# Seven RMS norms on one NeuronCore: the last square summed on its own, one root for four PSUM banks, weight parts moved, and most unread products of TensorE left out

## The chip, the cores and the metric

One Trainium2 chip, one of its NeuronCores. The metric is the device time of one launch in microseconds; lower is better. TensorE multiplies, VectorE and ScalarE do the elementwise work, SyncE issues the loads.

## The reference, cut to what matters

Two networks of two layers each follow one another on 512 rows of 1024 features (a context of 256 rows runs beside the first one). All is float32. The norms that this case is about are these:

```python
# first block, per layer l (modulate = RMS norm over the 1024 features, gain, scale and shift)
x = x + gt1 * merge_branches(...)                                  # w_o
x = x + gt2 * sq_relu_mlp(modulate(x, g_norm2[l], sh2, sc2), w_ff1[l], w_ff2[l])
...                                                                # the same for ctx_s in layer 0
# second block, per layer
h = _rmsnorm(x, pre_mix_g[layer]);  h = mixer(h)
x = x + _rmsnorm(h, post_mix_g[layer])
h = _swiglu(_rmsnorm(x, pre_ffn_g[layer]), w_gate, w_up, w_down)
x = x + _rmsnorm(h, post_ffn_g[layer])

def _rmsnorm(x, g):
    y = x * lax.rsqrt(jnp.mean(x * x, axis=-1, keepdims=True) + EPS)
    return y * g
```

A norm needs every feature of a row before it gives its first value, so each of them stands between two stretches of products.

## The kernel before, in words

Activations lie with their features on the 128 partitions: `x` is eight blocks (`KB` = 8) of 128 features by 512 rows, `xc` the same with 256 rows. A float32 product is made of three: each operand is split into a rounded upper part and a lower part, and `three` multiplies upper by upper, upper by lower and lower by upper. Weights come as tiles of 128x1024, in the order in which they are used. Four buffers hold them (`R` = 4): SyncE loads `raw`; ScalarE writes `w_hi` (`split(c)` does it for tile c + 3); VectorE writes `w_lo` (`lower_w(c)`, also for tile c + 3), which frees `raw` for the next load; TensorE then multiplies the tile into one of the four PSUM banks of `ring` (`product`, L1681 to L1683). Each engine runs its own instruction list in order and waits on semaphores; `plan()` fixes the order of the steps.

A norm after a stretch of products goes like this. The last tile of the stretch is added to `x` by VectorE (`residual`, L3006, or L3382 in the second block's feed-forward part). VectorE squares the block (L2655), adds the square to the running sum in `scr` block 2 (L2656) and tells TensorE (`squares_done`, L2659). TensorE sums over the partitions by one-column products: for each of four slices of 128 rows the slice of `scr` is the stationary operand and a column of ones the moving one (`column_sums`, L1752; in `last_norm` L2266 and in `mixed_norm` L2283 the sum and the last square are summed by products of their own, two groups of four). The profile counts each float32 product of this kind as two. ScalarE takes four roots, one for each slice's bank (`column_roots`, L932). VectorE takes the reciprocal (L2609). TensorE spreads it over the partitions by four products with the identity (`spread_rstd`, L1759). VectorE scales the first block (L2637, L3318 or L3100), ScalarE writes its upper part, VectorE its lower part (L2645, L3322), and the first product of the next stretch follows; the other blocks follow in the same pipeline.

While the chain of small steps runs, TensorE is given products that nobody reads (`keep_warm`, L1724, 128x512 each). `WARM`, `WARM_MIXED` and `WARM_POST` say how many stand before the sums, after them, and after the spread.

The places, in order of time (us of the profiled execution, end of the last product before the norm):

- 293: `norm2` of the context, layer 0 (`column_norm`, 256 rows). TensorE also has to sum and spread what `x`'s first norm needs here (L1802, L1740).
- 892 and 1683: `norm2` of the main rows, layers 0 and 1 (`column_norm`).
- 2040: `pre_mix` of layer 0 (`column_norm`).
- 2239 and 2868: `post_mix` (`mixed_norm`). Here ScalarE squares the tiles itself (L1091) and copies them (L1092), then splits the next weight tile (L894), loads the table of the root (`root_table`, L936) and takes the roots.
- 2610: `post_ffn` of layer 0 (`last_norm`), and 3238: `post_ffn` of layer 1, with which the kernel ends.

Two more sums stand between products: in `kv_norm1` (1272) and before the main rows' first norm ("roots", 485).

The loops of `w_o` and of `ff` on VectorE are hardware loops (`grouped`), with addresses worked out in registers in `w_o`.

```python
for kind, layer, stream, first in steps: ...
    elif kind == "post_ffn":           last_norm(first, ring[:, 0, :] if layer else bank[0])
    elif kind in ("norm2", "pre_mix"): column_norm(first, length(stream), summed(kind, layer, stream), bank[0], stream == "ctx")
    elif kind == "post_mix":           mixed_norm(layer, first)
```

Of the kernel before, what the change touches and what calls it, by code (L numbers as in the profile page):

```python
# [6 lines left out]
F32 = mybir.dt.float32  # L7
# [57 lines left out]
WARM, WARM_MIXED, WARM_POST = (11, 4, 8), (0, 9, 11), (2, 9, 11)  # L65
# [3 lines left out]
PAD = 16  # L69

# [308 lines left out]
def build(nc, ws, vecs, mats, ropes, x_in, ctx_in, bv_in, out, upto=None):  # L379
# [5 lines left out]
    with ExitStack() as stack:  # L385
# [42 lines left out]
        bank = [stack.enter_context(nc.psum_tensor(f"bank{i}", [P, SEQ], F32)) for i in range(4, 8)]  # L428
# [454 lines left out]
        def _(act):  # L883
# [750 lines left out]
            for n, (kind, layer, stream, first) in enumerate(steps):  # L1634
# [20 lines left out]
                elif kind == "norm2":  # L1655
                    norm(layer, stream, first, 3)
                elif kind == "pre_mix":
                    gain_norm(first, layer == 0)
                elif kind in ("post_mix", "post_ffn"):
                    post_norm(first)  # L1660
# [15 lines left out]
        def _(pe):  # L1676
# [49 lines left out]
            def column_norm(first, T, is_summed, spread, with_x):  # L1726

                keep_warm(first, WARM[0])
                column_sums(T, is_summed, 2)
                keep_warm(first, WARM[1])  # L1730
                C.next(root_ready, T // P)
# [12 lines left out]
            def column_sums(T, is_summed, at_block, done=ss_ready):  # L1744
                for k in range(1 if is_summed else KB):
                    if is_summed:
                        pe.wait_ge(s_acc, C.next(s_acc))
                    else:
                        pe.wait_ge(sq_ready, C.next(sq_ready))
                    src = scr[:, at_block if is_summed else k % 2, :]  # L1750
                    for tt in range(T // P):
                        m = nc.tensor.matmul(bank[tt][:, 0:1], src[:, tt * P:(tt + 1) * P], ones[:, 0:1],  # L1752
                                             start=k == 0, stop=is_summed or k == KB - 1)
                    m.then_inc(done, 1)
# [12 lines left out]
            def first_mod():  # L1767
# [9 lines left out]
                for t in range(FIRST):  # L1777
# [11 lines left out]
                    if t == KB + 3:  # L1789
                        pe.wait_ge(s_bv, 16)  # L1790
                        column_sums(CTX, True, 0)
                        C.next(root_ready, CTX // P)
# [43 lines left out]
            def kv_norm1(first):  # L1836
# [5 lines left out]
                column_sums(SEQ, True, 2)  # L1842
                C.next(root_ready, SEQ // P)
# [416 lines left out]
            def last_norm(first, spread):  # L2260

                keep_warm(first, WARM_POST[0])
                for part in range(2):
                    pe.wait_ge(s_acc, C.next(s_acc))
                    for tt in range(4):
                        m = nc.tensor.matmul(bank[tt][:, 0:1], scr[:, 2 + part, tt * P:(tt + 1) * P], ones[:, 0:1],  # L2266
                                             start=not part, stop=bool(part))
                m.then_inc(ss_ready, 1)
                keep_warm(first, WARM_POST[1] if first < n_tiles else 3)
                C.next(root_ready, 4)  # L2270
# [4 lines left out]
            def mixed_norm(layer, first):  # L2275
# [11 lines left out]
                C.next(root_ready, 4)  # L2287
# [31 lines left out]
            def ml_in(first):  # L2319
                four_abreast(first)  # L2320
                column_sums(SEQ, True, 2)
                C.next(root_ready, 4)
# [12 lines left out]
            def ffn(layer, first):  # L2335
                four_abreast(first)
                for u in range(4, FFN_TILES):
# [3 lines left out]
                    if pos < 2 * n:  # L2341
                        product(c, SEQ, h_hi, h_lo)
                        if u == 4:
                            column_sums(SEQ, True, 2)
                            C.next(root_ready, 4)
# [155 lines left out]
            for kind, layer, stream, first in steps:  # L2501
# [4 lines left out]
                elif kind == "roots":  # L2506

                    pe.wait_ge(root_ready, C.now(root_ready))
                    column_sums(length(stream), True, summed_at(kind, layer, stream), s_ctx_sum)
                    C.next(root_ready, length(stream) // P)  # L2510
                elif kind == "post_ffn":
                    last_norm(first, ring[:, 0, :] if layer else bank[0])
                elif kind in ("norm2", "pre_mix"):

                    column_norm(first, length(stream), summed(kind, layer, stream), bank[0], stream == "ctx")
# [29 lines left out]
        def _(dve):  # L2545
# [54 lines left out]
            def column_rstd(T, kept=None):  # L2600
                if kept is None:
                    dve.wait_ge(root_ready, C.next(root_ready, T // P))
# [7 lines left out]
                C.next(s_rstd)  # L2610
                dve.wait_ge(s_rspread, C.next(s_rspread))
# [37 lines left out]
            def add_squares(src, T, start=False, at_block=2):  # L2649
# [6 lines left out]
                step(nc.vector.tensor_tensor(total, total, scr[:, 3, :T], ALU.add))  # L2656

# [351 lines left out]
            def w_o(layer, stream, first):  # L3009
                T = length(stream)  # L3010
                step(nc.vector.memset(scr[:, 2, :T], 0.0))

                def body(c, u, off):
                    lower_w(c, off)
                    add_squares(residual(c, u, off, off, layer, stream, 2), T)
                grouped(dve, KB, first, body, C, {post: R, dve_own: 2 * R})
                squares_done()

            def ff(layer, stream, first):
# [54 lines left out]
                def body(c, u, off, between=None):  # L3074
# [17 lines left out]
                else:  # L3092
                    grouped(dve, 64, first, body, C, {evac: KB, dve_own: 4 * KB - 1, post: 2 * KB}, size=16)
                squares_done()
# [16 lines left out]
            def mix_out(layer, first):  # L3111
# [10 lines left out]
                lower_w(first + KB)  # L3122
# [190 lines left out]
            def residual_parts(i, first, mixed, gain):  # L3313

                column_rstd(SEQ)
# [23 lines left out]
            def ffn(layer, first):  # L3339
# [4 lines left out]
                dve.wait_ge(root_ready, C.next(root_ready, 4))  # L3344
# [20 lines left out]
                for u in range(4, FFN_TILES):  # L3365
                    c = first + u
                    pos, n = (u % 24, 8) if u < 48 else (u - 48, 6)
                    if u > 6:
                        lower_w(c)
                    done(c)  # L3370
# [10 lines left out]
                    else:  # L3381
# [3 lines left out]
                        elif u >= 48:  # L3385
                            squares_done()
                            step(nc.vector.tensor_tensor(scr[:, 3, :], z[:, m, :], z[:, m, :], ALU.mult))
                squares_done()
# [19 lines left out]
            def ml_in(first):  # L3408
                i = deferred("ml_in", 1)
                lower_w(first)  # L3410
# [3 lines left out]
                dve.wait_ge(root_ready, C.next(root_ready, 4))  # L3414
# [217 lines left out]
            for kind, layer, stream, first in steps:  # L3632
# [5 lines left out]
                elif kind == "norm1" and (layer, stream) == (0, "ctx"):  # L3638
                    dve.wait_ge(root_ready, C.next(root_ready, CTX // P))
                    norm(0, "ctx", 0)  # L3640
                    step(nc.vector.tensor_copy(v_bias[:, :], bias_columns))
                elif kind == "roots":
                    C.next(root_ready, length(stream) // P)
# [57 lines left out]
```

## Time and profile before

| | |
|---|---|
| median of 3 runs | 3254.96 us (3254.74 to 3256.89) |
| time of the profiled execution | 3257.88 us |
| its span | 3256.1 us |
| TensorE products | 3191.3 us busy, 98% of the span, 16081 instructions |
| TensorE weight loads | 2682.4 us, 82% |
| VectorE | 2096.6 us, 64% |
| ScalarE | 1236.7 us, 38% |
| mean granted clock of TensorE | 0.991 of full speed |

The span is what the profiler saw from the first instruction to the last; 1.8 us of the launch lie outside it. "Busy" of TensorE counts the unread products and the weight loads that its products wait for, so 98% is not work that the reference asks for.

### The profile page before, as it was taken

How to read it: one execution, taken by the hardware profiler on the slowest of the kernel's cores; microseconds unless marked ns; L12 is line 12 of the kernel's file. 1: busy time of each engine (PE TensorE's matmuls, PEld its weight loads, DVE VectorE, ACT ScalarE, POOL GpSimd, SP SyncE). 2: the span in 40 equal slices, each digit the busy share in tenths (PEclk: the TensorE clock that was granted, in tenths of full speed). 3: DMA queues.
4: the chain of work that ended last, by engine and by line, in shares of the span. 5: the costliest groups of instructions: out<-in, count | busy, mean ns of one | idle time of the engine just before them, and what ended most of it. 6: DMA issues, size and time to landing. Idle time of an engine off the chain costs nothing.

```text
span 3256.1 us, 42822 instructions
## 1 busy us (share of the span) xinstructions
PE 3191.3 (98%) x16081; PEld 2682.4 (82%) x16081; DVE 2096.6 (64%) x2925; ACT 1236.7 (38%) x1828; POOL 0.2 (0%) x4
## 2 busy tenths in 40 slices
PE   8899999999999999999999999999999999999998
PEld 6889998887888888888788888888888878888886
DVE  6777886655687778656475655875544676664446
ACT  4654435454232223555332222535222266542221
POOL 0000000000000000000000000000000000000000
PEclk9999999999999999999999999999999999999999
DMA  7654552211334553211222222222222336223222
GB/s 270 198 188 155 179 189 89 68 56 65 116 130 136 173 185 114 100 56 52 78 84 97 101 98 95 80 97 78 97 93 98 107 71 88 69 77 105 97 97 72
DMA packets 100716, 358.18 MB, mean 110 GB/s; under 512 B 11208, under 2 KB 12368, under 8 KB 100560
## 3 DMA queue, kind: packets, MB, share of 16 engines
q1 hardware_dynamic: 98864, 352.85, 31.7%
q10 hardware_dynamic: 1696, 3.16, 2.0%
q8 instruction: 108, 1.77, 0.2%
q14 instruction: 48, 0.39, 0.0%
HBM read 351.76 MB, written 2.10 MB: 109 GB/s over the span
## 4 chain that ended last, share of the span: by engine, by line
PE 90%; DVE 5%; ACT 2%; issue 1%; DMA 0%; DVEq 0%; ACTq 0%; SPq 0%
PE ring L1681 26%; PE ring L1683 25%; PE ring L1682 25%; PE bank L1681 2%; PE bank L1683 2%; PE bank L1682 2%; DVE w_lo L2576 1%; ACT w_hi L894 1%; PE ring L2009 1%; PE ring L2010 1%; PE bank L2034 1%; PE bank L2035 1%; PE ring L1980 1%; DVE x L3327 0%; PE bank L2165 0%
## 5 line engine op out<-in xcount | busy, mean ns | idle before, releaser
L1681 PE MATMUL ring<-h_hi,w_hi 128*128 128x512 f32 (+1 forms) x2776 | 1028.7, 371 | 16.3 <-DVE h_lo L2645 8.5
L1683 PE MATMUL ring<-h_hi,w_lo 128*128 128x512 f32 (+1 forms) x2776 | 1020.3, 368 | 0.0
L1682 PE MATMUL ring<-h_lo,w_hi 128*128 128x512 f32 (+1 forms) x2776 | 1020.3, 368 | 0.0
L2576 DVE TENSOR_TENSOR w_lo<-raw,w_hi 128x1024 fp32r<-128x1024 f32 x598 | 730.8, 1224 | 319.2 <-ACT w_hi L894 301.8
L894 ACT ACTIVATE w_hi<-raw 128x1024 fp32r<-128x1024 f32 x598 | 630.4, 1056 | 707.9 <-PE ring L1683 667.5
L1681 PEld LDWEIGHTS ring<-h_hi,w_hi 128*128 128x128 f32 x2776 | 529.5, 191 | 109.8 <-issue 14.4
L1683 PEld LDWEIGHTS ring<-h_hi,w_lo 128*128 128x128 f32 x2776 | 528.6, 190 | 86.0
L1682 PEld LDWEIGHTS ring<-h_lo,w_hi 128*128 128x128 f32 x2776 | 529.6, 191 | 82.8
L1681 PE MATMUL ring<-y_hi,w_hi 128*128 128x512 f32 (+1 forms) x1456 | 540.0, 371 | 11.7 <-DVE z L2860 7.7
L1683 PE MATMUL ring<-y_hi,w_lo 128*128 128x512 f32 (+1 forms) x1456 | 536.3, 368 | 0.0
L1682 PE MATMUL ring<-y_lo,w_hi 128*128 128x512 f32 (+1 forms) x1456 | 536.0, 368 | 0.0
L1681 PEld LDWEIGHTS ring<-y_hi,w_hi 128*128 128x128 f32 x1456 | 275.8, 189 | 60.9 <-DVE z L2860 10.2
L1683 PEld LDWEIGHTS ring<-y_hi,w_lo 128*128 128x128 f32 x1456 | 275.9, 189 | 45.6
L1682 PEld LDWEIGHTS ring<-y_lo,w_hi 128*128 128x128 f32 x1456 | 276.0, 190 | 44.1 <-issue 0.5
L1596 ACT ACTIVATE scr<-ring 128x512 f32<-128x512 f32 (+1 forms) x96 | 50.5, 526 | 302.7 <-PE ring L1683 300.1
L3081 DVE TENSOR_TENSOR z<-scr 128x512 f32<-128x512 f32 (+1 forms) x96 | 57.4, 598 | 125.4 <-ACT scr L1596 125.1
L3006 DVE SCALAR_TENSOR_TENSOR x<-ring,mod,x 128x512 f32<-128x512 f32 (+1 forms) x80 | 60.0, 751 | 118.4 <-PE ring L1683 118.4
L2882 DVE TENSOR_REDUCE mx<-ring 128x1 fp32r<-128x768 f32 (+1 forms) x80 | 67.9, 849 | 61.9 <-PE ring L2010 61.4
L2892 DVE TENSOR_TENSOR y_lo<-z,y_hi 128x512 fp32r<-128x512 f32 (+1 forms) x112 | 72.2, 646 | 48.9 <-ACT y_hi L1507 47.8
L1133 ACT ACTIVATE scr<-scr 128x512 f32<-128x512 f32 x40 | 25.3, 632 | 196.6 <-DVE scr L3374 196.6
L1507 ACT ACTIVATE y_hi<-bank 128x512 fp32r<-128x512 f32 (+1 forms) x112 | 63.4, 566 | 75.0 <-PE bank L1683 74.0
L1500 ACT ACTIVATE z<-bank 128x512 f32<-128x512 f32 (+1 forms) x112 | 63.6, 568 | 54.8 <-PE bank L2035 52.5
(382 smaller groups left out, 3104.0 us busy)
## 6 DMA issues: line engine op xcount, KB each, us to landing
raw<-ws SPq DMA_DIRECT2D x606, 512.0 KB, 3.3
z<-ws SPq DMA_DIRECT2D x52, 512.0 KB, 4.4
x<-ws SPq DMA_DIRECT2D x4, 512.0 KB, 9.7
x<-x_t SPq DMA_DIRECT2D x1, 2048.0 KB, 11.3
out_t<-x SPq DMA_DIRECT2D x8, 256.0 KB, 2.0
z<-xc ACTq DMA_DIRECT2D x6, 256.0 KB, 11.3
xc<-ctx_t SPq DMA_DIRECT2D x1, 1024.0 KB, 12.7
z<-ropes ACTq DMA_DIRECT2D x2, 512.0 KB, 4.3
```

Of the source, the lines that this page charges most:

```text
L894: nc.scalar.activation(w_hi[:, t % R, :], raw[:, t % R, :], ACT.Copy).then_inc(w_hi_ready, 1)
L1500: nc.scalar.activation(z[:, 13 + k % 2, :T], bank[k % 2][:, :T], ACT.Exp, scale=HEAD ** -0.5)\
L1507: nc.scalar.activation(y_hi[:, 4 + k % 2, :T], bank[k % 2][:, :T], ACT.Exp, scale=HEAD ** -0.5)\
L1596: nc.scalar.activation(scr[:, u % 2, :T], ring[:, c % R, :T], ACT.Relu).then_inc(evac, 1)
L1681: nc.tensor.matmul(o, a_hi, b_hi, start=start, stop=False)
L1682: nc.tensor.matmul(o, a_hi, b_lo, start=False, stop=False)
L1683: return nc.tensor.matmul(o, a_lo, b_hi, start=False, stop=stop)
L2576: nc.vector.tensor_tensor(w_lo[:, u, :], raw[:, u, :], f(w_hi[:, u, :]), ALU.subtract).then_inc(w_ready, 1)
L2882: nc.vector.reduce_max(mx[:, h % 2, qt:qt + 1], view[:, 0:n_kt * P], AX_X).then_inc(s_max, 1)
L2892: nc.vector.tensor_tensor(y_lo[:, b, :T], src, f(y_hi[:, b, :T]), ALU.subtract).then_inc(s_p, 1)
L3006: step(nc.vector.scalar_tensor_tensor(o, ring[:, c % R, :T], g, o, ALU.mult, ALU.add), post)
L3081: step(nc.vector.tensor_tensor(z[:, m % 2, :T], scr[:, m % 2, :T], scr[:, m % 2, :T], ALU.mult))
```

## The change: what it does, and the diff

1. **Last square.** In `w_o`, in `ff` and in the feed-forward part `ffn`, the last block's square is no longer added to the sum. `last_squares` writes it to `scr` block 3 and signals; `squares_done` is moved ahead of the last residual. TensorE sums block 2 and block 3 by products of their own (`part_sums`, twice), the first group before the last square is there.
2. **One root.** The four banks become one PSUM tensor, and `column_roots` is one instruction over a column of each bank, with one increment of `root_ready`.
3. **Weight parts.** In `post_mix`, `root_table` moves ahead of the wait for the last tile, and `split(first)` moves behind the root. In `residual_parts`, `lower_w(first)` stands between the reciprocal and the wait for the spread.
4. **Unread products.** `WARM` goes from (11, 4, 8) to (0, 0, 4), `WARM_MIXED` from (0, 9, 11) to (0, 0, 5), `WARM_POST` from (2, 9, 11) to (0, 0, 5), and the three after the last sums of the kernel become one: 155 products before, 30 after.
5. **`w_o`** is written out instead of looped, and its sum starts with the first square instead of a memset.

```diff
-WARM, WARM_MIXED, WARM_POST = (11, 4, 8), (0, 9, 11), (2, 9, 11)
+WARM, WARM_MIXED, WARM_POST = (0, 0, 4), (0, 0, 5), (0, 0, 5)
+FF_SQUARES = 7
...
-        bank = [stack.enter_context(nc.psum_tensor(f"bank{i}", [P, SEQ], F32)) for i in range(4, 8)]
+        banks = stack.enter_context(nc.psum_tensor("bank4", [P, 4, SEQ], F32))
+        bank = [banks[:, i, :] for i in range(4)]
...
             def column_roots(T, cols=root_cols):
-                for tt in range(T // P):
-                    nc.scalar.activation(cols[:, tt:tt + 1], bank[tt][:, 0:1], ACT.Sqrt, bias=eps[:, 0:1],
-                                         scale=1.0 / D).then_inc(root_ready, 1)
+                n = T // P
+                nc.scalar.activation(cols[:, 0:n].rearrange("p (a b) -> p a b", b=1), banks[:, 0:n, 0:1], ACT.Sqrt,
+                                     bias=eps[:, 0:1], scale=1.0 / D).then_inc(root_ready, 1)
...
-            def post_norm(first):
-                root_table()
+            def post_norm(first, mixed):
+                if not mixed:
+                    root_table()
                 act.wait_ge(ss_ready, C.next(ss_ready))
                 column_roots(SEQ)
+                if mixed:
+                    split(first)
...
                     if layer or u:
                         split(c)
+                    if u == KB - 1:
+                        root_table()
                     done(c)
...
-                split(first + KB)
...
-            def column_norm(first, T, is_summed, spread, with_x):
+            def column_norm(first, T, squares_before, spread, with_x):
+                part_sums(T, 2, squares_before, True, False)
                 keep_warm(first, WARM[0])
-                column_sums(T, is_summed, 2)
+                part_sums(T, 3, 1, False, True).then_inc(ss_ready, 1)
                 keep_warm(first, WARM[1])
...
+            def part_sums(T, at_block, after, start, stop):
+                pe.wait_ge(s_acc, C.next(s_acc, after))
+                for tt in range(T // P):
+                    m = nc.tensor.matmul(bank[tt][:, 0:1], scr[:, at_block, tt * P:(tt + 1) * P], ones[:, 0:1],
+                                         start=start, stop=stop)
+                return m
...
# kv_norm1, and the same for "roots"
                 product(first, CTX, h_hi, h_lo, before=blocks_ready(k0))
-                column_sums(SEQ, True, 2)
+                part_sums(SEQ, 2, FF_SQUARES, True, False)
+                part_sums(SEQ, 3, 1, False, True).then_inc(ss_ready, 1)
...
             def last_norm(first, spread):
+                part_sums(SEQ, 2, 1, True, False)
                 keep_warm(first, WARM_POST[0])
-                for part in range(2): ...
+                m = part_sums(SEQ, 3, 1, False, True)
                 m.then_inc(ss_ready, 1)
-                keep_warm(first, WARM_POST[1] if first < n_tiles else 3)
+                keep_warm(first, WARM_POST[1] if first < n_tiles else 1)
...
-            def column_rstd(T, kept=None):
+            def column_rstd(T, kept=None, between=None):
...
                 nc.vector.reciprocal(rstd_cols[:, :T // P], roots[:, :T // P]).then_inc(s_rstd, 1)
                 C.next(s_rstd)
+                if between:
+                    between()
                 dve.wait_ge(s_rspread, C.next(s_rspread))
...
+            def last_squares(src, T):
+                nc.vector.tensor_tensor(scr[:, 3, :T], src, src, ALU.mult).then_inc(s_acc, 1)
...
             def w_o(layer, stream, first):
                 T = length(stream)
-                step(nc.vector.memset(scr[:, 2, :T], 0.0))
-                def body(c, u, off):
-                    lower_w(c, off)
-                    add_squares(residual(c, u, off, off, layer, stream, 2), T)
-                grouped(dve, KB, first, body, C, {post: R, dve_own: 2 * R})
-                squares_done()
+                for u in range(KB):
+                    lower_w(first + u)
+                    if u < KB - 1:
+                        add_squares(residual(first + u, u, 0, 0, layer, stream, 2), T, start=u == 0)
+                    else:
+                        squares_done()
+                        last_squares(residual(first + u, u, 0, 0, layer, stream, 2), T)
...
# ff, tile 15 of each group of 16; ffn, its last tile, likewise
+                        if m == 2 * KB - 1:
+                            squares_done()
                         o = residual(c, m - KB, off, 0, layer, stream, 5)
-                        add_squares(o, T, start=m == KB)
+                        if m == 2 * KB - 1:
+                            last_squares(o, T)
+                        else:
+                            add_squares(o, T, start=m == KB)
...
# residual_parts (VectorE); mix_out and ml_in lose their own lower_w
-                column_rstd(SEQ)
+                column_rstd(SEQ, between=lambda: lower_w(first))
```

## Rows read from the trace of the kernel before

**Rows 1.** The page's head: span and instructions.

```profile
span 3256.1 us, 42822 instructions
```

**Rows 2.** Groups by line: busy us, mean ns of one, idle before it and releaser.

```profile
L932 ACT ACTIVATE small<-bank,eps 128x1 f32<-128x1 f32 x50 | 9.1, 264 | 62.2 <-PE bank L1752 41.4 <-PE bank L2266 20.8
...
L2655 DVE TENSOR_TENSOR scr<-x 128x512 f32<-128x512 f32 (+1 forms) x72 | 49.8, 692 | 2.5
```

**Rows 3.** The chain, norm2 of layer 0: start us, us, what.

```profile
892.62 0.25 PE ring L1683
...
893.12 0.76 DVE x L3006
...
895.60 1.05 PE bank L1752 x8
...
897.73 1.17 PE bank L1759 x8
...
898.92 0.76 DVE scr L2637
```

**Rows 4.** The chain, pre_mix of layer 0.

```profile
2040.07 2.56 PE ring L1724 x11
...
2045.91 0.76 DVE scr L2637
```

**Rows 5.** The chain, post_mix of layer 0.

```profile
2240.27 0.59 ACT z L1092
2240.86 0.94 ACT w_hi L894
...
2241.82 1.28 ACT L936
...
2245.39 0.76 DVE z L3318
```

**Rows 6.** The chain, post_mix of layer 1.

```profile
2868.49 1.74 PE bank L2283 x16
...
2873.36 0.76 DVE z L3318
```

**Rows 7.** The chain, post_ffn of layer 0.

```profile
2610.10 0.25 PE ring L1683
...
2614.85 1.23 DVE w_lo L2576
...
2617.42 0.76 DVE z L3318
```

**Rows 8.** The chain, post_ffn of layer 1, the kernel's end.

```profile
3238.11 0.25 PE ring L1683
...
3243.41 0.75 DVE z L3100
```

**Rows 9.** The chain, norm2 of the context.

```profile
294.26 2.68 PE ring L1724 x11
...
298.75 0.89 PE bank L1740 x8
```

**Rows 10.** The chain, the last add before "roots" and the sums in kv_norm1.

```profile
486.38 0.44 DVE scr L2656
...
1272.59 0.79 PE bank L1752 x8
```

**Rows 11.** Stretches: busy us by engine (instructions), then TensorE's granted clock, DMA share, GB/s.

```profile
2195.10:2198.50 3.40, 3.40 (x32) 3.40 (x32) 0.00 (x0) 0.37 (x1) 0.00 (x0) 1.00 0.00 0
2199.00:2202.40 3.40, 3.40 (x10) 2.62 (x9) 0.18 (x1) 1.55 (x3) 0.00 (x0) 0.50 0.00 0
...
2610.30:2620.60 10.30, 8.38 (x47) 6.36 (x45) 5.64 (x9) 2.91 (x7) 0.00 (x0) 1.00 0.31 103
...
1277.40:1280.80 3.40, 1.08 (x5) 0.93 (x6) 3.27 (x5) 1.92 (x3) 0.00 (x0) 1.00 0.05 20
1280.80:1284.20 3.40, 3.40 (x10) 2.63 (x9) 3.40 (x7) 1.63 (x3) 0.00 (x0) 0.50 0.02 5
```

More of the change, by code:

```diff
@@ L1659, in _ @@
                 elif kind in ("post_mix", "post_ffn"):
-                    post_norm(first)
+                    post_norm(first, kind == "post_mix")
                 elif kind == "ab":
@@ L1742, in x_spread @@
                 m.then_inc(s_x_spread, 1)
[L1744 to L1754, printed above, removed]
+            def part_sums(T, at_block, after, start, stop):
[4 more added lines that the diff above has]
+                return m
             def spread_rstd(T, spread):
@@ L1790, in first_mod @@
                         pe.wait_ge(s_bv, 16)
[L1791 to L1792 removed]
+                        part_sums(CTX, 0, 1, True, True).then_inc(ss_ready, 1)
+                        C.next(root_ready)
                         nc.tensor.matmul(bias_columns, bias_rows, ident[0:8, 0:8], start=True, stop=True)
@@ L2260, in last_norm @@
             def last_norm(first, spread):
+                part_sums(SEQ, 2, 1, True, False)
                 keep_warm(first, WARM_POST[0])
[L2263 to L2267, printed above, removed]
+                m = part_sums(SEQ, 3, 1, False, True)
                 m.then_inc(ss_ready, 1)
-                keep_warm(first, WARM_POST[1] if first < n_tiles else 3)
-                C.next(root_ready, 4)
+                keep_warm(first, WARM_POST[1] if first < n_tiles else 1)
+                C.next(root_ready)
                 spread_rstd(SEQ, spread)
@@ L2286, in mixed_norm @@
                 keep_warm(first, WARM_MIXED[1])
-                C.next(root_ready, 4)
+                C.next(root_ready)
                 spread_rstd(SEQ, bank[0])
@@ L2320, in ml_in @@
                 four_abreast(first)
-                column_sums(SEQ, True, 2)
-                C.next(root_ready, 4)
+                part_sums(SEQ, 2, 1, True, True).then_inc(ss_ready, 1)
+                C.next(root_ready)
                 for u in range(4, 10):
@@ L2343, in ffn @@
                         if u == 4:
-                            column_sums(SEQ, True, 2)
-                            C.next(root_ready, 4)
+                            part_sums(SEQ, 2, 1, True, True).then_inc(ss_ready, 1)
+                            C.next(root_ready)
                         if u == 5:
@@ L2508, in _ @@
                     pe.wait_ge(root_ready, C.now(root_ready))
-                    column_sums(length(stream), True, summed_at(kind, layer, stream), s_ctx_sum)
-                    C.next(root_ready, length(stream) // P)
+                    part_sums(length(stream), 2, FF_SQUARES, True, False)
+                    part_sums(length(stream), 3, 1, False, True).then_inc(s_ctx_sum, 1)
+                    C.next(root_ready)
                 elif kind == "post_ffn":
@@ L2513, in _ @@
                 elif kind in ("norm2", "pre_mix"):
-                    column_norm(first, length(stream), summed(kind, layer, stream), bank[0], stream == "ctx")
+                    column_norm(first, length(stream), 1 if kind == "norm2" else FF_SQUARES, bank[0], stream == "ctx")
                 elif kind == "post_mix":
@@ L3092, in ff @@
                 else:
-                    grouped(dve, 64, first, body, C, {evac: KB, dve_own: 4 * KB - 1, post: 2 * KB}, size=16)
-                squares_done()
+                    grouped(dve, 64, first, body, C, {evac: KB, dve_own: 4 * KB - 3, post: 2 * KB}, size=16)
             def post_norm(gain_of):
@@ L3343, in ffn @@
                     lower_w(first + u)
-                dve.wait_ge(root_ready, C.next(root_ready, 4))
+                dve.wait_ge(root_ready, C.next(root_ready))
                 nc.vector.reciprocal(rstd_cols[:, :], root_cols[:, :]).then_inc(s_rstd, 1)
@@ L3413, in ml_in @@
                     lower_w(first + u)
-                dve.wait_ge(root_ready, C.next(root_ready, 4))
+                dve.wait_ge(root_ready, C.next(root_ready))
                 nc.vector.reciprocal(rstd_cols[:, :], root_cols[:, :]).then_inc(s_rstd, 1)
@@ L3638, in _ @@
                 elif kind == "norm1" and (layer, stream) == (0, "ctx"):
-                    dve.wait_ge(root_ready, C.next(root_ready, CTX // P))
+                    dve.wait_ge(root_ready, C.next(root_ready))
                     norm(0, "ctx", 0)
@@ L3642, in _ @@
                 elif kind == "roots":
-                    C.next(root_ready, length(stream) // P)
+                    C.next(root_ready)
                 elif kind == "norm1":
```

14 lines of the change are left out of this document (6 added, 8 removed).

## The prediction, made before the changed kernel had run

> **What bounds the kernel now.** I read the page's head first, for the span [rows 1]; then the groups by line, for what a root and a square cost [rows 2]; then the chain of waits around each norm, because a mean over the kernel says nothing of places that take 8 us each. The reader is to see one pattern there: the last product ends, a chain of small steps crosses VectorE, TensorE, ScalarE, VectorE, TensorE, VectorE, and only then the next product can start. Outside the norms TensorE multiplies without a gap, so a microsecond taken out of such a chain is a microsecond of the kernel, and a microsecond anywhere else is nothing. Last I read the stretches in which TensorE's granted clock was low [rows 11].
>
> Where the chain shows L1724, TensorE ran unread products while it had nothing else. A step that follows such a piece by 0.04 us was in general released by another engine, not by TensorE. Norm2 of the context is different: eleven unread products fill 294.26 to 296.94, and its sums stand behind them in TensorE's list [rows 9].
>
> **The change part by part.** Durations are those of one execution, of 3257.88 us, whose span is 3256.1 [rows 1]; the median of the runs is 3254.96, 2.9 us under it. The sum is a difference, made against the profiled execution and then taken off the median.
>
> The new chain, from the end of the last product to VectorE's first scaling, for 512 rows: 0.04 for the wait, residual 0.76 [rows 3], wait 0.02, square 0.70 [rows 2], 0.06 to TensorE, four slices summed 1.05 [rows 3], 0.08 to ScalarE, one root 0.26 [rows 2], 0.03, reciprocal 0.19, 0.04, spread 1.17 [rows 3], 0.02. That is 4.42 us. One root over four banks isn't in the trace: at least the 0.26 of one bank, at most the 0.7 of four in a row; I take 0.26, because it still writes so few columns.
>
> - Norm2 of both layers: in layer 0 the last product ends at 892.87 and the scaling starts at 898.92, 6.05 us [rows 3]. Gone are the add with its wait, the loop's end and its address registers (together 1.2) and three roots (0.45). Gain 1.6, and the same in layer 1: **3.2**.
> - Pre_mix: 2040.07 to 2045.91, 5.84 us [rows 4]; `ff` had no address registers on this way. **1.4**.
> - Post_mix of layer 0: the square and the copy (0.59) of the last tile lead to 2240.86; then ScalarE splits a weight tile (0.94) and loads the root's table (1.28) before it takes the roots, and VectorE scales at 2245.39 [rows 5]. The last product ended about 0.5 us before the copy began at 2240.27, at 2239.75, so this is 5.64. In the new order the table load lies under the products of the last tile, since ScalarE has nothing to do there; without that cover it costs its 1.28 again. ScalarE squares (0.6), TensorE sums (to 1.7), the root is there at 2.0. Now something else is late: ScalarE splits until 3.1, and VectorE, which has taken `lower_w(first)` in ahead of its wait for the spread, works on it until 4.33 (1.23 for such a piece [rows 7]). The spread is ready at 3.5 and waits. 4.35, gain **1.3**. Queued behind the piece on VectorE are the scalings, so the whole next stretch waits for it.
> - Post_mix of layer 1: the table was loaded already, and the way was 2868.49 to 2873.36, 4.87 us [rows 6]. The new one is the same 4.35: **0.5**.
> - Post_ffn of layer 0: from 2610.35 to 2617.42, 7.07 us [rows 7]. `lower_w` stood ahead of the reciprocal here, which had to wait for 2616. Sixteen records of sums become eight behind the last square. New: root at 2.8, split until 3.9, VectorE's piece until 5.13, scaling at 5.15. **1.9**.
> - Post_ffn of layer 1: 3238.36 to 3243.41, 5.05 us [rows 8]; new 4.33. **0.7**.
> - Norm2 of the context: from the end of L1802 at 294.26 to the end of the spread at 298.75, 4.5 us [rows 9]. With 256 rows each step is about half: two groups of sums 1.0, root and reciprocal 0.6, spread 0.55. Gain **2.3**, most of it the unread products that stood in the way.
> - "Roots": the add of 0.44 [rows 10] with its wait and the loop's end go from VectorE's way to the first norm of the main rows. **0.7**.
> - Kv_norm1: here the sums stand between two tiles of products and the squares were long there. A second group of eight records costs TensorE its 0.8 [rows 10] to 0.9. **Minus 0.9**.
>
> The deferred norms of `ffn` and `ml_in` get one root for four, with TensorE at products meanwhile: nothing. The writing-out of `w_o` but for its last tile, and the adds that `ff` saves in its first three groups, lie under products of 5.5 us a tile: nothing. The next load of a weight tile waits for `lower_w`; its transfer is needed many products later and is hidden before and after.
>
> Sum: 3.2 + 1.4 + 1.3 + 0.5 + 1.9 + 0.7 + 2.3 + 0.7 − 0.9 = 11.1 us.
>
> **What the missing unread products cost.** The granted clock never fell in one of the changed places: across the longest of them, post_ffn of layer 0, TensorE was busy for 8.38 of 10.30 us, and the clock stayed at full [rows 11]. It fell elsewhere: after 3.4 us in which TensorE ran only one-column sums (32 records) the next 3.4 us were at half, 1.2 instead of 2.4 GHz; and after 3.4 us with 1.08 us of work (a spread's end and five records in all) it fell as well [rows 11]. In a slow stretch TensorE made ten products, at 0.43 us each; at full clock they are 0.23, so a slow stretch that lies wholly on products costs about 1.7 us (fifteen would have fitted).
>
> After the change, the way from the last product to the spread holds nothing but one-column sums for 3.2 us (norm2, pre_mix, post_ffn), 2.3 us (post_mix) and about 2.4 us (context). Then come the spread and its four or five unread products, some 2 us at work. Behind them the first product still waits for VectorE and ScalarE's first block: 1.7 us at norm2 and pre_mix, 3.2 at post_mix and post_ffn. So each of seven places has one or two stretches like those [rows 11]. The lower bound is nothing: the clock holds. The upper is two slow stretches each, 3.3 us. At norm2 and pre_mix a fall would mostly lie on the spread and on waiting, with 0.5 to 1 us to pay; behind post_mix and post_ffn it would lie on products. I take 0.9 us a place: about four full slow stretches in all, 4 × 1.65 = 6.6, less what is hidden. **Minus 6.3.** The rows nearest to it (3.4 us of sums, and 2.3 us of idling in 3.4, both followed by a fall) are a little longer than most of the new gaps, hence not seven.
>
> The clock fell behind both such stretches [rows 11]. By the Trainium skill ("TensorE: Matmul & The Clock Gate", Part 1: The HAM clock gate) the throttled state is the default and only activity releases it. Taken alone, that rule speaks against this change: it would have all seven places fall once, 7 × 1.65 = 11.6 instead of 6.3, and the sum would be 0.5 us slower.
>
> Net: 11.1 − 6.3 = 4.8 us faster. Against the profiled 3257.9 that is 3253.1; against the median, 3254.96 − 4.8 = **3250.2 us**.
>
> **The rivals.**
> 1. The clock holds in most places (none to two falls). For it: the products just before and after each place are dense, and a place that was idle for 2 us of 10 kept its clock. Against it: the falls, both in the same rows [rows 11]. Then 8 to 11 us are gained: **3245**.
> 2. The clock falls everywhere, in some places for two stretches. Mechanism: the gap slows the spread to half, TensorE finds too little to do in the slow stretch itself and stays slow into the next products. It decides from 11.1 / 7 = 1.6 us a place: below that the change gains, above it loses. With two stretches at half of the places, 11 × 1.65 = 18: 7 us slower, **3262**. With one each: 3255.5, no change. For it, the fall after 1.08 us of work in 3.4 [rows 11]; against it, that the spread and its four or five unread products stand in the middle of each gap.
> 3. The chain gets shorter on paper only: ScalarE's one root over four banks costs as much as four (7 × 0.45 = 3.2), and the piece of `lower_w` comes later than I put it. Then the gain is about 8 gross, less the clock's 6.3: **3253**.
>
> **How the numbers follow.** The forecast (three to five falls, 3 to 7 us gained) 0.52; rival 1 0.25; rival 2 0.13, of which 0.05 at the slow end; rival 3 0.10. 0.2% is 6.5 us, about what a measurement of this kernel can tell from no change. Faster than 3248.4: rival 1 and the forecast's best tenth, 0.33. Slower than 3261.5: rival 2's end and a little for what I don't see, 0.06. The rest, 0.61, lies within. The range of 8 in 10 goes from rival 1 (3244.5) to the one-fall-each case with its spread (3257).
>
> **What would show it.** In the changed kernel's chain: sums starting 1.6 us after the last product of norm2 (2.7 before); one L932-like root of 0.26 per norm; scaling 4.4 us after the last product at norm2 and pre_mix, 4.35 at both post_mix, 5.15 at post_ffn of layer 0; at post_mix and post_ffn VectorE's w_lo piece as the last link ahead of the scaling; 16 records of sums in kv_norm1. In the granted clock: about four low stretches more than now, with products of 0.43 us behind post_mix and post_ffn. I am wrong if the new places show no low stretch (then it is rival 1), if slow products follow all of them (rival 2), or if a scaling starts later than said although the clock held (rival 3).

## The result and the profile after

The changed kernel took 3260.81 us in the median of 22 runs (3248.45 to 3267.41), the kernel before 3254.91 (3253.07 to 3258.85, 22 runs). The ratio is 1.0014, with a 95% interval of 1.0007 to 1.0020: slower by 0.14%. Measured once more with the experiments it took 3255.19 us (12 runs, 3248.68 to 3262.59) beside 3255.07, ratio 1.0003 (0.9993 to 1.0013). Both lie under the 0.2% that the prediction called the limit of what can be told from no change; faster it is not, and 4.8 us faster was forecast. One run of kernel 2 below (8154.78 us) and one of the kernel before (8256.51 us) stand far outside all others and count in no ratio or mean.

The runs of the changed kernel spread over 19 us (14 in the second set), those of before over 6 (7 to 12 beside the later experiments). Each run lists its span and the mean granted clock of TensorE, from which its time at the low clock follows: (1 − clock) × 2 × span. In the runs of the kernel before that were made beside the experiments it is 52 to 65 us nearly always, with a mean of 57; in those of the changed kernel 78 to 131 us, mean 111 (mean 99 in the second set). Over 21 of the 22 runs (one lists a clock that no time fits) a straight line, 3223.7 us + 0.32 × the time at the low clock, follows the run's time with a correlation of 0.97. Both kept profiles of the changed kernel are of quick runs: 3253.18 us with 98 us at the low clock, and 3248.68 with 78 in the second set. No run with the 117 us of the median was profiled. What follows is the first of the two. The page's head, its line of products and its line of roots:

```profile
span 3251.4 us, 42456 instructions
...
PE 3177.9 (98%) x15996; PEld 2676.0 (82%) x15996; DVE 2084.6 (64%) x2904; ACT 1231.8 (38%) x1792; POOL 0.2 (0%) x4
```

```profile
L936 ACT ACTIVATE small<-bank,eps 128x4 f32<-128x4 f32 (+1 forms) x14 | 3.7, 263 | 58.4 <-PE bank L1757 57.1 <-PE bank L2286 1.3
```

One root over four banks takes 263 ns, as one over a single bank did [rows 2]. The chain of waits at norm2 of layer 0, which answers to [rows 3] (start us, us, what):

```profile
887.70 0.24 PE ring L1691
887.94 0.02 issue
887.97 0.76 DVE x L3016
...
888.75 0.70 DVE scr L2666
889.45 0.14 issue
889.59 1.34 PE bank L1757 x8
...
891.50 0.14 issue
891.63 2.06 PE bank L1764 x8
...
893.72 0.76 DVE scr L2643
...
896.15 0.76 PE ring L1689
...
900.33 0.32 PE ring L1689
```

The sums begin 1.65 us after the last product, as the prediction had it. But the spread takes 2.06 us instead of 1.17, the sums 1.34 instead of 1.05, and the scaling starts 5.78 us after the last product: 4.42 were forecast, 6.05 it was. The granted clock tells why. Stretches of the changed kernel (columns as in [rows 11]):

```profile
886.80:890.10 3.30, 2.42 (x18) 2.17 (x17) 1.44 (x2) 0.00 (x0) 0.00 (x0) 1.00 0.50 159
890.30:893.50 3.20, 2.48 (x12) 2.42 (x13) 0.18 (x1) 0.26 (x1) 0.00 (x0) 0.50 0.00 0
893.70:896.90 3.20, 2.43 (x6) 1.45 (x6) 3.05 (x5) 1.58 (x3) 0.00 (x0) 0.50 0.00 0
897.10:900.30 3.20, 3.20 (x9) 2.48 (x8) 3.20 (x6) 1.76 (x3) 0.00 (x0) 0.50 0.02 5
```

The clock fell to 1.2 GHz while the one-column sums ran, stayed there through the spread and the gap behind it, and only rose when products had run for over 4 us, from 896.15 to 900.3, at 0.43 us each. That is one slow stretch of 10.2 us at one norm.

Where the clock held, or fell too late to matter, the chain is nearly what was forecast. Pre_mix, against [rows 4]:

```profile
2037.15 1.04 PE bank L1757 x8
...
2038.27 0.27 ACT small L936
...
2038.89 1.14 PE bank L1764 x8
2040.03 0.03 issue
2040.06 0.76 DVE scr L2643
```

From the last product at 2035.50 that is 4.56 us (before 5.84; forecast 4.42). TensorE, idle now, starts 0.14 us after its release, where 0.06 and 0.04 were forecast. Post_mix of layer 0, against [rows 5], 4.25 us from the last product at 2232.29, with VectorE's weight piece as the last link:

```profile
2232.29 1.75 PE bank L2286 x16
...
2234.23 1.05 ACT w_hi L898
...
2235.31 1.23 DVE w_lo L2580
2236.54 0.70 DVE z L3331
```

Post_mix of layer 1 took 4.26 us (against [rows 6]). The clock did fall at both, at 2235.0 and 2866.4 and for 3.4 us each, but behind the sums, and VectorE's weight piece ends after the slowed spread. In layer 0 the clock was back at 2238.4 and the first product started at 2239.71: that fall cost nothing. Post_ffn of layer 0 and the kernel's end, against [rows 7, 8]:

```profile
2601.47 0.70 DVE z L3397
...
2604.96 2.06 PE bank L1764 x8
2607.01 0.02 issue
2607.04 0.76 DVE z L3331
```

```profile
3234.64 1.40 PE bank L1757 x8
3236.04 0.64 PE ring L1732
3236.67 2.02 PE ring L1764 x8
3238.69 0.02 issue
3238.72 1.41 DVE z L3114 x2
```

At post_ffn of layer 0 the spread at the low clock ends at 2607.01 and has become the last link, in place of the weight piece; the scaling comes 5.6 us after the last product (forecast 5.15). At the end the scaling comes 5.67 us after the last product, later than the 5.05 of before, because sums and spread ran at the low clock. The one unread product runs there at about twice its time, but the reciprocal ends only at 3236.55 and the spread starts at once behind it (3236.60): the product isn't what holds the chain up. Kv_norm1 shows the second group of sums on TensorE (before 0.79, [rows 10]):

```profile
1267.75 1.68 PE bank L1757 x16
```

All stretches below 1 make 100 us in this profile, 62 in the one before.

### The profile page after: what moved, and what is told of

Its sections match the earlier page's. It is cut to its first block, busy times and chain, and to the rows that moved or that the text cites. A ratio compares the mean times of both kernels' runs of the same rounds, so it can differ in the third digit from the quotient of the medians.

```text
span 3251.4 us, 42456 instructions
## 1 busy us (share of the span) xinstructions
PE 3177.9 (98%) x15996; PEld 2676.0 (82%) x15996; DVE 2084.6 (64%) x2904; ACT 1231.8 (38%) x1792; POOL 0.2 (0%) x4
## 4 chain that ended last, share of the span: by engine, by line
PE 90%; DVE 5%; ACT 2%; issue 1%; DMA 0%; DVEq 0%; ACTq 0%; SPq 0%
PE ring L1689 26%; PE ring L1690 26%; PE ring L1691 26%; PE bank L1689 2%; PE bank L1691 2%; PE bank L1690 2%; DVE w_lo L2580 1%; ACT w_hi L898 1%; PE ring L2015 1%; PE ring L2016 1%; PE bank L2040 1%; PE bank L2041 1%; PE ring L1986 1%; PE bank L2171 0%; DVE z L2983 0%
## 5 line engine op out<-in xcount | busy, mean ns | idle before, releaser
L3016 DVE SCALAR_TENSOR_TENSOR x<-ring,mod,x 128x512 f32<-128x512 f32 x80 | 60.1, 751 | 121.0 <-PE ring L1691 121.0
```

The source lines that it names most:

```text
L3016: step(nc.vector.scalar_tensor_tensor(o, ring[:, c % R, :T], g, o, ALU.mult, ALU.add), post)
```

## The experiments

Two theories. A: the shorter chains are gained, and the granted clock takes it all back, because TensorE has too little to do at the norms. B: the loss lies in the other edits. Every kernel was timed beside the kernel before, whose medians were 3255.0 to 3255.6 us in the three sets. "Low" is the mean time at the low clock. Kernel 2 was timed in the first set only, 5 to 8 in the second, 9 to 11 in the third. Each interval is about 3 us wide to either side, so a difference between two kernels of less than about 4 us isn't told apart from none.

| kernel | unread products: WARM, MIXED, POST | median us | ratio to before (95%) | low us |
|---|---|---|---|---|
| before | (11, 4, 8), (0, 9, 11), (2, 9, 11) | 3255 | 1 | 57 |
| changed | (0, 0, 4), (0, 0, 5), (0, 0, 5) | 3260.8 / 3255.2 | 1.0014 / 1.0003 | 111 / 99 |
| 1, before + few | as changed | 3276.7 | 1.0069 (1.0055 to 1.0083) | 134 |
| 2, some kept | (3, 2, 8), (0, 2, 14), (3, 2, 14) | 3247.2 | 0.9974 (0.9965 to 0.9984) | 71 |
| 3, more kept | (5, 4, 8), (0, 4, 14), (5, 4, 14) | 3249.9 | 0.9983 (0.9974 to 0.9992) | 65 |
| 4, old counts | as before | 3260.4 | 1.0017 (1.0008 to 1.0027) | 70 |
| 5, four roots | as 2 | 3247.0 | 0.9975 (0.9966 to 0.9984) | 66 |
| 6, weight parts back | as 2 | 3253.1 | 0.9990 (0.9981 to 0.9999) | 76 |
| 7, add back | (11, 2, 8), rest as 2 | 3249.1 | 0.9982 (0.9973 to 0.9991) | 63 |
| 8, tail cut | (3, 2, 4), (0, 2, 5), (3, 2, 5) | 3251.6 | 0.9990 (0.9981 to 0.9999) | 82 |
| 9, head cut | (0, 0, 8), (0, 0, 14), (0, 0, 14) | 3254.0 | 0.9995 (0.9986 to 1.0003) | 94 |
| 10, context free | as 2, context (0, 1, 4) | 3246.9 | 0.9976 (0.9967 to 0.9986) | 69 |
| 11, longer tails | as 10, but 10, 17 and 17 behind the spread | 3246.7 | 0.9977 (0.9967 to 0.9987) | 67 |

The profiles give a second measure, which needs no median: how long TensorE makes no product of the program around a norm, from the start of the last product before it to the start of the first one behind it, in us. For kernel 10 at norm2 of layer 0 it is read so:

```profile
887.76 0.39 PE L1691 MATMUL ring<-h_hi,w_lo 128*128 128x512 f32 x1
...
895.04 0.47 PE L1689 MATMUL ring<-h_hi,w_hi 128*128 128x512 f32 x1 [0.61 <-DVE h_lo L2651]
```

| place | before | changed | kernel 4 | kernel 10 |
|---|---|---|---|---|
| norm2, context | 7.29 | 5.11 | 7.75 | 5.04 |
| norm2, layer 0 | 8.90 | 8.61 | 9.03 | 7.28 |
| norm2, layer 1 | 8.91 | 8.31 | 9.03 | 7.28 |
| pre_mix | 8.52 | 7.24 | 8.88 | 7.12 |
| post_mix, layer 0 | 9.26 | 7.81 | 8.47 | 7.77 |
| post_ffn, layer 0 | 10.70 | 9.22 | 10.86 | 8.59 |
| post_mix, layer 1 | 8.47 | 7.88 | 8.47 | 7.77 |
| sum | 62.1 | 54.2 | 62.5 | 50.9 |

**1. The counts alone.**

```diff
# on the kernel before
-WARM, WARM_MIXED, WARM_POST = (11, 4, 8), (0, 9, 11), (2, 9, 11)
+WARM, WARM_MIXED, WARM_POST = (0, 0, 4), (0, 0, 5), (0, 0, 5)
# and the three products after the last sums of the kernel become one
```

> The kernel before with edit 4 alone: the unread products cut from 155 to 30, nothing else. Theory A (the granted clock): the shorter chain of the other edits is really gained, about 11 us, and the missing unread products cost 14 to 18 us by more and longer stretches at 1.2 GHz. Then this kernel is 10 to 17 us slower than before (3265 to 3272; it still gains 1.5 us at the norm of the context, where unread products stood in the way), its time at the low clock is over 100 us, against 60 before, and its runs spread over 10 us or more. Theory B (the loss lies in the other edits, for instance in the weight piece that VectorE works on before the scaling, or in the root over four banks): this kernel is within 3 us of before.

21 us slower, more than theory A gave (10 to 17), and 134 us at the low clock. Theory B is out: this kernel has none of the other edits. Its chain at pre_mix, with the same steps as [rows 4]:

```profile
2045.92 0.14 issue
2046.06 1.85 PE bank L1752 x8
...
2049.06 2.06 PE bank L1759 x8
2051.12 0.02 issue
2051.14 0.76 DVE scr L2637
```

The clock had fallen at 2045.7, before the sums began. The last product ended at 2043.47 and the scaling started at 2051.14, 7.67 us later; before it was 5.84. Its gaps without products are longer than those of the changed kernel (10.35 against 7.24 us here), and the counts cost more here than there.

**2 and 3. The changed kernel with unread products that fit.**

```diff
# on the changed kernel; experiments 5, 6, 7, 10 and 11 start from this one
-WARM, WARM_MIXED, WARM_POST = (0, 0, 4), (0, 0, 5), (0, 0, 5)
+WARM, WARM_MIXED, WARM_POST = (3, 2, 8), (0, 2, 14), (3, 2, 14)
```

> The changed kernel with the idle stretches filled with as many unread products as fit without standing in the way: WARM (3, 2, 8), WARM_MIXED (0, 2, 14), WARM_POST (3, 2, 14). Theory A: the gain of the chain stays (about 10 us) and most of the falls are gone, 3244 to 3250, low clock 60 to 80 us. Theory B: no better than the changed kernel, 3257 or more.

> As the run with (3, 2, 8), but WARM (5, 4, 8), WARM_MIXED (0, 4, 14), WARM_POST (5, 4, 14): the products ahead of the sums and of the spread now delay them by about 0.5 us each. Theory A: no falls at the norms, the runs lie within 5 us of each other, and 4 to 6 us of the gain are paid back: 3246 to 3251. Theory B: 3257 or more.

Both as theory A had it. The first is 8.4 us faster than before; the second holds the clock better by 6 us, worth 1.9, and is 2.7 us slower, so by the medians it pays 4.6 for products that stand in the way. That is little more than the noise; the traces show 7.63 us without products at norm2 of layer 0 instead of 7.27. Chain and stretch of the first at norm2 of layer 0:

```profile
887.55 0.79 PE bank L1757 x8
888.33 0.81 PE ring L1732 x3
889.14 1.04 PE bank L1757 x8
...
890.75 0.04 issue
890.80 1.17 PE bank L1764 x8
...
891.99 0.76 DVE scr L2643
```

```profile
887.50:894.40 6.90, 6.27 (x38) 4.67 (x36) 3.90 (x7) 1.64 (x3) 0.00 (x0) 1.00 0.10 41
```

4.44 us from the last product to the scaling: the 4.42 of the forecast, once the clock is at full. Where its clock still fell (post_ffn of layer 0), fourteen unread products at the low clock held the first product back: 9.36 us without a product, 8.59 in kernel 10.

**4. The changed kernel with the old counts.** The edit is the reverse of that in 1, on the changed kernel.

> The changed kernel with the old counts (11, 4, 8), (0, 9, 11), (2, 9, 11). Eleven products ahead of the sums of the last square hold them back until 3.5 us after the last product, against 1.6 without them and 2.7 in the kernel before. Theory A: the clock holds, norm2 and pre_mix lose 0.5 us each against before, the other places keep their gain as far as nine products after the sums leave it: 3251 to 3256. Theory B: above 3257, as the other edits are all in it.

Slower than expected (3251 to 3256), with a clock nearly as good as before. Eleven products now stand between the two groups of sums:

```profile
889.95 0.79 PE bank L1757 x8
890.73 2.66 PE ring L1732 x11
893.40 0.79 PE bank L1757 x8
894.18 1.03 PE ring L1732 x4
895.22 0.91 PE bank L1764 x8
896.12 0.02 issue
896.15 0.76 DVE scr L2643
```

The chain is TensorE's alone, 6.20 us, longer than the 6.05 of before [rows 3], and over the seven places the gain is gone (62.5 us without products, 62.1 before). Kv_norm1 costs its 0.9 on top. In its profile the clock also fell for 10.2 us in mlstm, far from the norms; from the first product behind post_ffn of layer 0 to the last one before post_mix of layer 1 it took 252.3 us against 247.5 before, so that fall cost about 4.9 us. The shorter chain and smaller counts belong together, so the cut as such was needed; its size was the mistake.

**5 to 7. One part undone at a time**, from kernel 2.

```diff
# 5: four roots, one increment after the last
-                nc.scalar.activation(cols[:, 0:n]..., banks[:, 0:n, 0:1], ACT.Sqrt, ...).then_inc(root_ready, 1)
+                for tt in range(n):
+                    m = nc.scalar.activation(cols[:, tt:tt + 1], bank[tt][:, 0:1], ACT.Sqrt, ...)
+                m.then_inc(root_ready, 1)
...
# 6: the order of before
                 root_table()                       # in post_norm, always; no longer in mix_out
...
+                split(first + KB)                  # end of mix_out, ScalarE; lower_w(first + KB) on VectorE
-                column_rstd(SEQ, between=lambda: lower_w(first))
+                column_rstd(SEQ)                   # lower_w(first) ahead of it in ml_in
...
# 7: norm2, pre_mix, roots, kv_norm1
-                part_sums(T, 2, squares_before, True, False)
                 keep_warm(first, WARM[0])
-                part_sums(T, 3, 1, False, True).then_inc(ss_ready, 1)
+                part_sums(T, 2, 1, True, True).then_inc(ss_ready, 1)
...
-                            last_squares(o, T)
+                            add_squares(o, T)
```

> The kernel with counts (3, 2, 8), (0, 2, 14), (3, 2, 14), with edit 2 undone: four roots instead of one over four banks (one increment after the last). If one root over four banks costs what a single one does, as the prediction took it: 0.45 us at each of six places of 512 rows and 0.25 at two of 256 on the way, 2.5 to 4 us slower than with one root. If it costs as much as four (rival 3): no change, within 1 us.

> The same with edit 3 undone: the table load and the weight piece back ahead of the root in post_mix, the piece of VectorE ahead of the reciprocal in post_ffn of layer 0. By the prediction's sums: 0.9 of the 1.3 at post_mix of layer 0, nearly nothing at post_mix of layer 1, 1.3 of 1.9 at post_ffn, so 2 to 3.5 us slower. If VectorE's piece before the scaling eats what the earlier spread gives: within 1 us.

> The same with edit 1 undone at norm2, pre_mix, the roots and kv_norm1: the last square is added to the sum and summed by one group, with eleven unread products ahead of it as before. The add (0.72 at 512 rows, 0.46 at 256) comes back at five places, the loop's end at two, and kv_norm1 wins back 0.9: 2 to 4 us slower.

Four roots: no slower in the median (3247.0 against 3247.2), which missed the expectation. In the trace they are there, `2037.75 0.73 ACT small L937 x4` at pre_mix against one of 0.27, and the time without products is longer by what was forecast: 7.73 us at norm2 of layer 0 (7.27 in kernel 2), 7.58 at pre_mix (7.11), 8.22 at post_mix of layer 1 (7.77 in kernel 10). So the gain of 0.45 at a place is real. Over all places it is about 2.9 us; the runs had 5 us less at the low clock, which by the slope of 0.32 makes up for 1.6, and the rest is smaller than the medians can tell. Weight parts back: 5.9 us slower, more than 3.5; at post_mix of layer 0 the scaling comes 6.1 us after the last product instead of 4.3. About 0.9 of that is the clock, which had fallen there (a spread of 2.09 us instead of 1.17), so the whole of the 5.9 isn't the order's. Add back: 1.9 us slower, just under the expected 2 to 4 and within the noise; norm2 and pre_mix are without products for 8.07 us instead of 7.3 and 7.1.

**8 and 9. Which of the two idle stretches drops the clock.**

> Counts (3, 2, 4), (0, 2, 5), (3, 2, 5): as many unread products as fit ahead of the spread, but behind it no more than the changed kernel has. It tells which idle stretch drops the clock. If it is mainly the one before the spread, which the changed kernel left with one-column sums alone: 3246 to 3250, as with 8 and 14. If it is mainly the one behind it: 3253 to 3259, low clock over 90 us.

> Counts (0, 0, 8), (0, 0, 14), (0, 0, 14): nothing ahead of the sums and of the spread, as in the changed kernel, but all that fits behind the spread. The counterpart of (3, 2, 4), (0, 2, 5), (3, 2, 5). If the clock falls for the stretch ahead of the spread, and most of the loss is there: 3254 to 3259 with 90 to 110 us at the low clock. If both stretches count alike: 3250 to 3253, 80 us.

Cutting behind the spread costs 4.4 us over kernel 2 and adds 11 us at the low clock; cutting ahead of the sums and of the spread costs 6.8 us and adds 23. Both together (the changed kernel, in the same set as 9) add 28 us and 8 us of time. So both matter: the tail came out between its two cases, the head at the lower edge of its first. That the one ahead matters more holds for the time at the low clock (94 against 82 us); the two medians can't be told apart. And the 6.8 us aren't the price of the head alone: where the clock has fallen, the full tail stands in the way. At norm2 of layer 0 seven unread products took 2.99 us behind the slow spread, and TensorE was without products of the program for 9.40 us, against 8.61 in the changed kernel with its four. With products kept ahead of the spread, the changed kernel's few behind it leave it 3.5 us faster than before.

**10 and 11. Towards a better kernel.**

```diff
-                keep_warm(first, WARM[0])
+                keep_warm(first, 0 if with_x else WARM[0])
-                keep_warm(first, WARM[1])
+                keep_warm(first, 1 if with_x else WARM[1])
# 11 also
-WARM, WARM_MIXED, WARM_POST = (3, 2, 8), (0, 2, 14), (3, 2, 14)
+WARM, WARM_MIXED, WARM_POST = (3, 2, 10), (0, 2, 17), (3, 2, 17)
```

> Counts (3, 2, 8), (0, 2, 14), (3, 2, 14), but none ahead of the context's last square and one after it. There the three products end later than the square is ready and hold the sums back by about 0.6 us. 0.5 to 1 us faster than with them, 3246 to 3247, if the clock doesn't fall there more often.

> As the kernel with none ahead of the context's last square, with 10, 17 and 17 instead of 8, 14 and 14 products behind the spread, up to what still ends before the first product is ready. If the falls that are left come from the idle stretch behind the spread: 1 to 3 us faster and about 60 us at the low clock. If they come from elsewhere (mlstm, the fronts), or if the longer tails hold the first product back: no change or up to 2 us slower.

3246.9 and 3246.7: no difference from kernel 2 that could be told. The low stretches that are left in the profile of 10 lie in the first 500 us, at 1003 and 1078, at kv_norm1 (1272), in the mixer (2187) and at the kernel's end, not at the norms between.

The second run of the changed kernel had this on record:

> The changed kernel as it is, beside the others on one chip: 3257 to 3263, with 90 to 130 us at the low clock.

It came out at 3255.19, under the 3257 expected, with 99 us at the low clock instead of 111. By the slope that is 3.9 us of the 5.6 between the two sets.

## Why the prediction was wrong

- **The chain: right.** The steps were forecast at 11.1 us. At the full clock the scaling came 4.56 us after the last product at pre_mix (4.42), 4.25 and 4.26 at post_mix (4.35); kernel 2 shows 4.44 at norm2. The context's spread ended 2.3 us after L1807 (2.2), kv_norm1 paid its 0.9. Where the clock held (kernel 10), the seven places of the table gave 11.2 us; for these seven the forecast had 10.6. Kernels 2, 10 and 11 really are 8 us faster, with 10 to 14 us more at the low clock than before.
- **One root for the price of one: right** (263 ns), worth the forecast 0.45 us at a place by kernel 5's traces; rival 3 is out. Its worth in the median is too small to tell.
- **Where it failed: "I take 0.9 us a place: about four full slow stretches in all ... Minus 6.3."** The term was mis-sized. The mean time at the low clock rose by 54 us, as much as sixteen stretches of 3.4 us, and at 0.32 us for each of the 54 that costs 17 (second set: 42 us, 13). Even in the quick run that was profiled the falls cost more than 6.3. Estimates from its rows, against kernel 10: norm2 of layer 0 3.3 us (1.3 more without products, and ten slow products at 2.0 more), norm2 of layer 1 1.0, post_ffn of layer 0 2.3, the kernel's end 1.3 (against the forecast chain of 4.33), both post_mix 0.1 together: about 8. Another 4.0 come from a fall of 10.2 us in mlstm, for which the prediction had no term. Where the rest of the mean's 17 lies no kept trace shows.
- **What the term missed.** First, at norm2 and pre_mix it priced a whole fall, spread and all, at 0.5 to 1 us. At 1.2 GHz the sums take up to 1.40 and the spread 2.06 us in the changed kernel, instead of 1.05 and 1.17, on the way that sets the end. Second, one fall isn't one stretch: at norm2 and at post_ffn of layer 0 it lasted 10.2 us; behind its start TensorE was busy for 2.48 and 2.43 of 3.20 us, and the clock stayed down into the products. Third, the places were mixed up: behind post_mix a fall was to lie on products, but there it lay on the spread and the unread products and cost nothing. The prediction's own rival 2 names the mechanism, down to the break-even of 1.6 us a place; it got 0.13.
- **Rows 11 read too kindly.** Both stretches there had been followed by a fall, and the prediction took four of seven because most new gaps are "a little" shorter. The clock "never fell in one of the changed places" was also too much: in the profile of before it fell at 489 and 1280.9, behind "roots" and kv_norm1, which edit 1 touches. In the changed kernel's profile six of eight places hold a fall (890, 1682, 2235, 2604, 2866, 3235), in its second profile seven. By the Trainium skill ("TensorE: Matmul & The Clock Gate", Part 1: The HAM clock gate) the throttled state is the default and activity releases it. These traces agree with it as far as they go: at norm2 of layer 0 the clock fell when the products had stopped and came back after 4 us of them. The sum by that rule, no change, was nearer than mine.
- **The spread of the runs** wasn't forecast. The two profiles of the changed kernel differ in their places (the context only in the second, mlstm only in the first) and in how long the falls last (norm2 of layer 0: 10.2 and 6.8 us). That such differences make up the 19 us is what the line over the runs says; no trace of a slower run shows it.

## What to carry to other kernels

Where a chain of small steps interrupts the products, count its idle stretches again whenever the chain gets shorter, and size the unread products to each gap: too many stand in the way (kernel 4, +13 us over kernel 2), too few let the clock fall (the changed kernel, +8 to 14 us). Price a fall by what the low clock does to the chain and to the next products, not by one stretch. Too many behind the spread also cost once the clock has fallen, since they then take twice their time (kernels 2 and 9). And look at the clock of every run, not only at the median: it explained the spread that the median hid.

## What the runs showed of the hardware that wasn't expected

- Busy time in the profile doesn't tell whether the clock is kept. At norm2 of layer 0 TensorE counts as busy for 2.42 of the 3.30 us ahead of the fall in the changed kernel, part of it with one-column sums (L1757: eight records in 1.04 us at pre_mix); in kernel 2, with thirteen unread products in 6.9 us, it is 6.27, and the clock stayed at 1.00.
- An idle TensorE starts 0.14 us after what released it; with unread products running it starts 0.04 us after (ahead of the spread: 891.50 in the changed kernel against 890.75 in kernel 2). The unread products also hide this wake-up, in the kernel before at the sums as well (0.04 at 895.55).
- The clock fell in a place that nobody touched. Mlstm around 2808 to 2819 ran at the full clock before, and in the changed kernel's profile at half:

```profile
2808.50:2818.60 10.10, 9.28 (x33) 7.92 (x32) 4.43 (x8) 1.95 (x4) 0.00 (x0) 0.50 0.00 0
```

From the first product behind post_ffn of layer 0 to the last one before post_mix of layer 1 the changed kernel took 253.2 us, the kernel before 247.5; 1.7 of the difference are the slow products at its start, so this fall cost 4.0 us. Such a fall stands in seven of the thirteen profiles that aren't of the kernel before (3.4 to 10.2 us long), in those with few and with many unread products, kernels 1 and 4 among them. So a part of the loss doesn't come from the norms. What decides it there stays open; it wasn't tried.
